# Output panels 2 to 15 multiplied in pairs by Strassen's scheme, with y's sums of tokens and x' made during the branch panels

## What is computed

```python
    x = first_block(...)                      # ends in rms_norm(x) * final_norm_g
    # second block
    ua = (ya * silu(za)) @ w_branch_a;  ub = ... @ w_branch_b;  uc = ... @ w_branch_c
    g = sigmoid(gate_logits.reshape(b, s, 3, D_MODEL))
    y = g[:, :, 0] * ua + g[:, :, 1] * ub + g[:, :, 2] * uc
    return x + y @ w_out
```

## Time and profile before

| | us |
|---|---|
| median of 3 runs | 2179.81 |
| lowest, highest | 2178.41, 2181.3 |
| the profiled execution | 2179.51 |
| its span, first to last instruction | 2178.1 |
| TensorE busy | 2145.9 (99% of the span) |
| VectorE busy | 1505.6 (69%) |
| ScalarE busy | 959.8 (44%) |
| gate pairs | about 697 to 1123 |
| branch panels | about 1840 to 2001 |
| output panels | about 2001 to 2178 |

### The profile page before, as it was taken

How to read it: one execution, slowest core, us unless ns; L and a number is a source line. 1 busy time by engine, 2 the same in 40 slices (tenths; PEclk the granted TensorE clock), 3 DMA queues, 4 the chain that set the end, 5 groups by cost and what they waited for, 6 DMA issues and landing times.

```text
span 2178.1 us, 34635 instructions
## 1 busy us (share of the span) xinstructions
PE 2145.9 (99%) x11672; PEld 1825.9 (84%) x11672; DVE 1505.6 (69%) x2524; ACT 959.8 (44%) x1631; POOL 60.6 (3%) x115
## 2 busy tenths in 40 slices
PE   8899999999999999999999999999999999999999
PEld 6788888788888999999997777778777888888887
DVE  5887877785658888888866666665767766665333
ACT  7533454433335444444444555555656554222221
POOL 0000000000000000000000000000000000000000
PEclk9999999999999999999999999999999999999999
DMA  9676523674443443343332222222222223554443
GB/s 356 238 262 224 182 95 99 226 268 142 146 144 131 144 141 125 121 141 129 118 112 88 87 87 87 87 87 78 74 82 68 88 88 117 169 168 152 145 145 112
DMA packets 83508, 302.21 MB, mean 139 GB/s; under 512 B 9285, under 2 KB 11717, under 8 KB 75217
## 3 DMA queue, kind: packets, MB, share of 16 engines
q1 hardware_dynamic: 71568, 258.24, 35.2%
q0 software_dynamic: 9104, 38.28, 5.1%
q10 hardware_dynamic: 2738, 4.47, 0.5%
HBM read 279.69 MB, written 21.26 MB: 138 GB/s over the span
## 4 chain that ended last, share of the span: by engine, by line
PE 78%; DVE 7%; ACT 5%; DVEq 4%; issue 3%; DMA 3%; ACTq 1%; SPq 0%
PE bank L417 18%; PE bank L419 18%; PE bank L418 18%; PE bank L1147 6%; PE bank L1149 6%; PE bank L1148 6%; DVE w_lo L411 3%; DMA w_raw<-stream 2%; ACT w_hi L401 2%; PE bank L540 1%; PE bank L571 1%; DVEq L406 1%; PE bank L553 1%; ACT L461 1%; ACT probs L614 1%
## 5 line engine op out<-in xcount | busy, mean ns | idle before, releaser
L417 PE MATMUL bank<-x_hi,w_hi 128*128 128x512 f32 x2224 | 886.2, 398 | 6.9 <-DVEq L668 1.9
L419 PE MATMUL bank<-x_hi,w_lo 128*128 128x512 f32 x2224 | 866.7, 390 | 0.0
L418 PE MATMUL bank<-x_lo,w_hi 128*128 128x512 f32 x2224 | 866.2, 389 | 0.0
L411 DVE TENSOR_TENSOR w_lo<-w_raw,w_hi 128x512 fp32r<-128x512 f32 x524 | 363.0, 693 | 495.0 <-ACT w_hi L401 473.6
L401 ACT ACTIVATE w_hi<-w_raw 128x512 fp32r<-128x512 f32 x524 | 331.2, 632 | 666.4 <-PE bank L419 554.0
L417 PEld LDWEIGHTS bank<-x_hi,w_hi 128*128 128x128 f32 x2224 | 417.6, 188 | 110.8 <-issue 11.1
L418 PEld LDWEIGHTS bank<-x_lo,w_hi 128*128 128x128 f32 x2224 | 417.9, 188 | 89.6 <-issue 6.0
L419 PEld LDWEIGHTS bank<-x_hi,w_lo 128*128 128x128 f32 x2224 | 417.5, 188 | 88.2
L1147 PE MATMUL bank<-x_hi,pw_hi 128*128 128x256 f32 x1176 | 332.9, 283 | 0.3 <-DVE pw_lo L1914 0.3
L1148 PE MATMUL bank<-x_lo,pw_hi 128*128 128x256 f32 x1176 | 332.8, 283 | 0.0
L1149 PE MATMUL bank<-x_hi,pw_lo 128*128 128x256 f32 x1176 | 332.8, 283 | 0.0
(11 more groups left out here) (193 smaller groups left out, 1812.0 us busy)
## 6 DMA issues: line engine op xcount, KB each, us to landing
w_raw<-stream SPq DMA_DIRECT2D x262, 512.0 KB, 3.8
pw_raw<-stream SPq DMA_DIRECT2D x84, 512.0 KB, 4.6
wmod<-w_mod_rows SPq DMA_DIRECT2D x32, 1024.0 KB, 7.1
front_raw<-stream SPq DMA_DIRECT2D x16, 1024.0 KB, 9.3
wmod<-w_mod_rows POOLq DMA_DIRECT2D x16, 1024.0 KB, 5.7
sig_store<-logits POOLq DMA_DIRECT2D x45, 256.0 KB, 2.5
sig_back<-sig_store SPq DMA_DIRECT2D x8, 768.0 KB, 5.6
gate_sig<-sig_store SPq DMA_DIRECT2D x7, 768.0 KB, 5.7
```

What stands on the lines that cost most here:

```text
L411: nc.vector.tensor_tensor(w_lo[:, q, :], raw_quarter(s), w_hi[:, q, :].bitcast(F32), ALU.subtract).then_inc(lo_ready, 1)
L417: nc.tensor.matmul(bank_ap[:, :tokens], hi, x_hi[:, kx, :], start=start, stop=False)
L418: nc.tensor.matmul(bank_ap[:, :tokens], hi, x_lo[:, kx, :], start=False, stop=False)
L419: return nc.tensor.matmul(bank_ap[:, :tokens], lo, x_hi[:, kx, :], start=False, stop=stop)
```

## The change

Output panels 0 and 1 stay as they were. Panels 2 to 15 are multiplied in 7 pairs by the same `product` that the gate pairs use, so the last stage is 2 panels and 49 products.

What the pairs need is made as follows. The sums of y's token blocks are made in place in x3: `sums_of_y(k)` for k = 0 to 6 stands in step 1 of the odd beats 3, 5, ... 15, and k = 7 at the start of the output stage; each is four VectorE operations of 128 x 256. They are split into x2 (8 ScalarE and 8 VectorE operations of 128 x 1024) during output panels 0 and 1. x' of tiles 2 to 15 is no longer made in the output stage: in each beat n = 2 to 15 SyncE loads x1's tile from DRAM into the one buffer `x_prime`, VectorE scales it there (`x_primed`, in step 2, behind branch(n, 0)), and GpSimd's queue stores it back to the same place. The load of tile n waits until tile n - 1 has been stored. Each result tile then takes two VectorE additions (`back_and`, and the bank).

```diff
-          ("gated", 4), ("branch", KT - 1), ("out", KT)]
+          ("gated", 4), ("branch", KT - 1), ("out", 2)]
...
+            def x_prime_load(n):
+
+                if n.lowest() > 2:
+                    sp.wait_ge(xp_stored, (n - 2).times(16).value())
                 else:
                     for stored in x1_stored:
                         sp.wait_ge(stored, 32)
+                sp.dma_start(x_prime[:, :], x_store[n.pick(), :, :].rearrange("a p t -> p (a t)")).then_inc(xp_loaded, 16)
+
+            def branch_loads(n, slot):
+
+                load_panel(sp, n + (FIRST["branch"] - 1))
+                sigmoid_loads(n, slot)
+                x_prime_load(n)
+            for slot in range(2):
+                branch_loads(At(2 + slot), slot)
+            with steps(sp, 1, KT // 2 - 1) as i:
+                for slot in range(2):
+                    branch_loads(At(2 + slot, 2, i), slot)
...
+            first = 4 * PAIRS
+            for n in range(2):
+                load_panel(sp, At(FIRST["out"] + n))
+            for n in range(2):
+                back_load(n)
+            for l in range(6):
+                load_factor(first + l)
+            sp.wait_ge(xp_stored, 16 * (KT - 2))
+            for p in range(OUT_PAIRS):
+                back_load(2 + 2 * p)
+                for l in range(4 * p + 6, min(4 * p + 8, 4 * OUT_PAIRS)):
+                    load_factor(first + l)
+                back_load(3 + 2 * p)
+                for l in range(4 * p + 8, min(4 * p + 10, 4 * OUT_PAIRS)):
+                    load_factor(first + l)
...
             panel(pe, At(g + 1), At(r + 1), x1_hi, x1_lo)
-            with steps(pe, 1, KT // 2) as i:
-                for n in range(2):
-                    panel(pe, At(g + n, 2, i), At(r + n, 2, i), x1_hi, x1_lo)
+            for l in range(PRODUCTS, PRODUCTS + 7 * OUT_PAIRS):
+                if l == PRODUCTS + 2:
+                    pe.wait_ge(t_ready, KT)
+                product(Factor(l))
...
+            g = FIRST["out"]
+            for s in range(8):
+                split_hi(act, At(4 * g + s))
+                token_sums_hi(KT // 2 + s)
+                if s == 5:
+                    store_result(0)
+                if s == 6:
+                    act.wait_ge(lo_ready, 4 * PANELS)
+                    factor_hi(Factor(PRODUCTS))
+                if s == 7:
+                    act.wait_ge(w_used, 4 * PANELS - 2)
+                    factor_hi(Factor(PRODUCTS + 1))
+            act.wait_ge(w_used, 4 * PANELS)
+            for l in range(PRODUCTS, PRODUCTS + 7 * OUT_PAIRS):
+                act_product(l)
+            store_result(KT - 1)
...
+            def x_primed(n):
+
+                dve.wait_ge(xp_loaded, (n - 1).times(16).value())
+                nc.vector.scalar_tensor_tensor(x_prime[:, :], x_prime[:, :], col("final_g", n), r_one[:, :],
+                                               ALU.mult, ALU.mult).then_inc(xp_made, 1)
+
+            def sums_of_y(k):
+
+                two = tile(x3, k.times(2) + 1)
+                one = tile(x3, k.times(2))
+                dve.drain()
+                nc.vector.tensor_tensor(one[:, HALF:], one[:, HALF:], one[:, :HALF], ALU.subtract)
+                dve.drain()
+                nc.vector.tensor_tensor(two[:, HALF:], two[:, HALF:], one[:, HALF:], ALU.subtract)
+                dve.drain()
+                nc.vector.tensor_tensor(two[:, :HALF], two[:, :HALF], two[:, HALF:], ALU.subtract)
+                nc.vector.tensor_tensor(one[:, :HALF], two[:, HALF:], one[:, :HALF], ALU.subtract)
+                dve.drain().then_inc(t_made, 1)
+
+            def branch_beat(n, slot, loaded, before, k=None):
 
                 for s in range(4):
...
+                    if s == 1 and k is not None:
+                        sums_of_y(k)
                     if s >= 2:
                         branch(n, s - 2, slot, loaded)
+                    if s == 2 and n.lowest() > 1:
+                        x_primed(n)
                     if s == 3:
                         low_part(n - 1, x1_hi, x1_lo, y_hi, y_split)
             branch_beat(At(1), 1, At(1), (0, None))
             with steps(dve, 0, KT // 2 - 1) as i:
                 branch_beat(At(2, 2, i), 0, At(1, 1, i), (1, At(1, 1, i)))
-                branch_beat(At(3, 2, i), 1, At(2, 1, i), (0, At(1, 1, i)))
+                branch_beat(At(3, 2, i), 1, At(2, 1, i), (0, At(1, 1, i)), At(0, 1, i))
...
+            def back_and(n, terms_so_far):
+
+                dve.drain()
+                dve.wait_ge(x_back_loaded[n % 2], 16 * (n // 2 + 1))
+                dve.wait_ge(result_stored[n % 2], 16 * (n // 2) + ONE)
+                nc.vector.tensor_tensor(result[:, n % 2, :].rearrange("p (a t) -> p a t", a=2), terms_so_far,
+                                        x_back[:, n % 2, :].rearrange("p (a t) -> p a t", a=2), ALU.add)
+                dve.drain()
+
+            def first_result(pair):
+
+                n = 2 + 2 * (pair.c - PAIRS)
+                back_and(n, pair_sum[:, :].rearrange("p (a t) -> p a t", a=2))
+                dve.wait_ge(product_done, 7 * pair.c + 5)
+                nc.vector.tensor_tensor(result[:, n % 2, :], result[:, n % 2, :], row_1[:, :], ALU.add).then_inc(row_read, 1)
+                dve.drain().then_inc(result_ready, 1)
...
+            sums_of_y(At(KT // 2 - 1))
+            for s in range(8):
+                split_lo(dve, At(4 * g + s))
+                if s > 0:
+                    token_sums_lo(KT // 2 + s - 1)
+                if s == 5:
+                    finish(0)
+                if s == 7:
+                    token_sums_lo(KT - 1)
+                    factor_lo(Factor(PRODUCTS))
+            weight_sum(Factor(PRODUCTS + 2))
+            factor_lo(Factor(PRODUCTS + 1))
+            for l in range(PRODUCTS, PRODUCTS + 7 * OUT_PAIRS):
+                dve_product(l)
+            second_result(At(PAIRS + OUT_PAIRS - 1), (PAIRS + OUT_PAIRS - 1) % 3)
...
+            with steps(pool, 0, KT - 2) as i:
+                n = At(2, 1, i)
+                pool.wait_ge(xp_made, (n - 1).value())
+                pool.dma_start(x_store[n.pick(), :, :].rearrange("a p t -> p (a t)"), x_prime[:, :]).then_inc(xp_stored, 16)
```

More of the change, by code:

```diff
@@ L53 @@
 PRODUCTS = 7 * PAIRS
+OUT_PAIRS = (KT - 2) // 2
 HALF = T // 2
@@ L994, in _ @@
             sigmoid_loads(At(1), 1)
-            with steps(sp, 0, KT // 2 - 1) as i:
-                for slot in range(2):
-                    load_panel(sp, At(FIRST["branch"] + 1 + slot, 2, i))
-                    sigmoid_loads(At(2 + slot, 2, i), slot)
-            def back_loads(n, slot, again=True):
-                src = x_store[n.pick(), :, :].rearrange("a p t -> p (a t)")
-                load_panel(sp, n + FIRST["out"])
-                if again:
-                    sp.wait_ge(result_ready, (n - 1).value())
+            def x_prime_load(n):
+                if n.lowest() > 2:
+                    sp.wait_ge(xp_stored, (n - 2).times(16).value())
                 else:
@@ L1907, in factor_lo @@
             def factor_lo(f):
-                if not f.exists():
+                if f is None:
                     return
@@ L2126, in finish @@
-                dve.wait_ge(result_stored[n.parity()], (n.half().times(16) + ONE).value())
-                nc.vector.tensor_tensor(result[:, n.parity(), :], acc[rr.parity()][:, :], back,
-                                        ALU.add).then_inc(result_ready, 1)
-                dve.drain().then_inc(acc_free[rr.parity()], 1)
-            def out_beat(n, peeled=False):
-                for s in range(4):
-                    split_lo(dve, (n + FIRST["out"]).times(4) + s)
-                    if s == 0 and not peeled:
-                        finish(n - 1)
@@ L2136, in _ @@
-            out_beat(At(0), peeled=True)
-            out_beat(At(1))
-            with steps(dve, 1, KT // 2 - 1) as i:
-                for slot in range(2):
-                    out_beat(At(slot, 2, i))
-            out_beat(At(KT - 2))
-            out_beat(At(KT - 1))
-            finish(At(KT - 1))
+                dve.wait_ge(w_used, 4 * (FIRST["out"] + n + 1))
+                nc.vector.tensor_tensor(result[:, n, :], acc[r % 2][:, :], back, ALU.add).then_inc(result_ready, 1)
+            def back_and(n, terms_so_far):
[5 more added lines that the diff above has]
+                dve.drain()
```

102 lines of the change are left out of this document (54 added, 48 removed).

## The result

The changed kernel takes 2216.5 us (2208.6 to 2217.4 in 4 runs) against 2179.2 (2178.4 to 2181.3 in 4): 1.014 times as long, with a 95% interval of 1.0119 to 1.0161. It is slower by 37 us, outside the predicted range of 2171 to 2197, near the time that rival B gives. The profiled execution took 2216.55 us, its span 2215.0.

A forecast was written before the change was run, and what follows sets the result against it. The prediction took TensorE as the bound: from the profiled 2179.5 us, -11.2 for products, +12.2 for the x' ring and +2.7 before the first product gave 2183.2, as a median 2183.5; range 2171 to 2197, likeliest 2178 to 2188.

The forecast's parts named there:

- rival B: Branch beats: x' stores land as x1's did, 4.8 us instead of 2.5; 2213 us, chance 0.1.
- What bounds the kernel now: Whole kernel: TensorE is most of the chain of waits; less matmul work is worth its full time unless something becomes late.
- Products instead of panels: Output stage: seven pairs at 2.88 us per product, 20.16 per pair against 21.76 for two panels; 11.2 us gained.
- Rival D: Output stage: products don't reach 2.88 us, 4.9 us lost per 0.1 us each; chance 0.18 together with C.
- The loop over x': Branch stage: 13 rings of waits through the one x' buffer take 154.0 us against 141.4 for 13 beats; TensorE loses 12.2.
- The ring: Branch beats: one x_primed to the next, via store and loads; 10.82 us even, 12.73 odd, against a beat of 10.88.
- From panels to products: Start of the output stage: TensorE ends its two panels and waits 2.7 us for factor 0; bounds 0.5 and 4.
- A: Branch beats: the ring doesn't bind, the half panel comes in time; 2171.3 us, chance 0.22 including rings losing under half.
- C: Branch beats: stores and loads cross, or GpSimd waits for VectorE's port; 2190 to 2193 us, chance 0.18 with D.

The follow-up runs named there:

- run 1: Changed kernel with SyncE issuing the first half of the next panel ahead of the x' load in each branch beat: 2178.9 us, 0.9994 of the kernel before.
- run 8: Changed kernel without an edit, profiled a second time: 2216.3 us, 1.0152 times the kernel before.
- run 2: Kernel before with only x' loaded, multiplied and stored back in the branch beats, in the changed kernel's order: 2202.0 us, 1.0092 times the kernel before.
- run 4: Changed kernel with x' made at the head of each branch beat, ahead of VectorE's four low splits: 2185.4 us, 1.0002 times the kernel before.
- run 5: Changed kernel with each branch beat's second half panel issued only when the first has landed, SyncE's loop written out: 2203.0 us, one run.

## Why the prediction was wrong

**What bounds the kernel now: right.** TensorE sets the time, less matmul work is worth its full length, and a wait in the branch stage costs its full length too.

**Products instead of panels: right.** 2.88 us per product was forecast. In run 1, 140.9 us from the first start to the last, 48.9 products: 2.88. In the changed kernel it is 142.4 / 48.9 = 2.91, with one stretch of 3.4 us at half clock, from 2069 (below). The same kernel in run 8 has no such stretch in its products and takes 140.9 again, so the stretch cost 1.5. Rival D is out. The first of each three matmuls in run 1, the changed kernel and run 8:

```profile
L1182 PE MATMUL bank<-x_hi,pw_hi x392: 278/283/388, 2037.9 to 2178.8; 128*128 128x256 f32 x196
```

```profile
L1176 PE MATMUL bank<-x_hi,pw_hi x392: 278/283/420, 2068.8 to 2211.2; 128*128 128x256 f32 x196
```

```profile
L1176 PE MATMUL bank<-x_hi,pw_hi x392: 283/283/387, 2071.8 to 2212.7; 128*128 128x256 f32 x196
```

**The loop over x': the mechanism was right, its size wrong, and this is the step that failed.** The term was +12.2, with bounds of 5.7 and 42 of which the range took in only the lower part; it measured +35.7. The ring binds, by the way the prediction went round it, and runs 1, 2 and 4 show it from three sides. The excess of 22.95 us over 154.0 splits over the 13 rings like this (sum of the forecast, sum measured):

| piece | forecast | changed kernel | excess |
|---|---|---|---|
| x' made to GpSimd's start | 3.8 | 9.3 | +5.5 |
| store landed, x' load issued | 34.7 | 31.1 | -3.6 |
| x' load issued to split of the half panel | 54.5 | 69.1 | +14.6 |
| split to next x' made | 61.1 | 67.5 | +6.4 |

- The store was right: from its start to SyncE's next issue it was 2.4 us on the mean where the forecast had 2.67. Rival B's time, 2213, was nearly right, but its cause, a store of 4.8, did not occur.
- GpSimd's start was taken from the earlier trace rows, where a store waited for ScalarE: 0.29. Here it is 0.66 to 0.94. The Trainium skill's rule of the shared port, which the prediction weighed, doesn't show: the store at 1918.43 began inside a split of VectorE's that ran from 1918.11 to 1918.80.
- The pair of x' load and half panel was taken from the earlier trace rows: 4.19. Here it is 5.31 on the mean: 0.71 from one issue to the other, where the row has 0.38, and 4.60 from there to the split, where it has 3.81. In the row the two halves were issued in 2.06 us. Here they take 0.91 in most odd rings, with 4.87 to the split on the mean, and 1.6 to 1.9 in the even ones, with 4.29, and the gates' load follows. With both behind the landing (run 5) the pair is 0.37 + 3.91 = 4.28, so the row was read rightly and carried over to a place where its condition didn't hold. In the odd rings the ring itself made that condition false: a late ring frees both halves before the first is issued. The estimate of 3.8 from the Trainium skill's formula, whose section describes transfers issued by GpSimd and not by SyncE, was further off than the row.
- The splits: 5.28 from the split to x' in odd beats instead of 4.83, and 3.12 instead of 2.92 in even ones without disturbance; the drain ahead of the sums (0.24 of idle time) was forgotten. From branch(n, 0) to x' it was 0.98 to 1.02 in all beats, where 0.85 was taken; the 0.80 that this leaned on stands in no row. In the changed kernel's even rings the way from the split to x' is up to 3.75, since the second split waits for TensorE, which the ring before had held up (0.44 at 1914.72).

How a size error of 15% in the ring became three times the loss: the forecast's even ring lay 0.06 under the beat, its odd one 1.85 over. What is lost is the ring less the beat. 1.77 us more on the mean ring, on an excess of 0.97, is all of it. The prediction saw for itself that 0.06 us per ring moved the result across 0.2% (it calls this a twentieth of B; it is a fortieth of B's 2.3). With every piece taken from an undisturbed place, 2178 to 2188 was too narrow a range for the likeliest case.

**From panels to products: right, 1.9 us instead of 2.7.** VectorE and ScalarE went as described, the split of the last sums waiting 3.34 behind the store; in run 1, where no ring holds up the panels ahead of it, TensorE's wait was 2.9. The end as a whole: -8.5 forecast, -6.5 in the changed kernel, -8.0 in the same kernel in run 8, -8.2 in run 1; the difference of 1.5 is that stretch at half clock.

**The first part: +7.8, put at nothing without a word, and open.** Without it the changed kernel would still be slower than the range: 2216.5 - 7.8 = 2208.7. Ahead of x1's first tile, 5.0 of 5.3 us are a longer wait of TensorE and, by the estimate above, a lowered clock; what makes the wait longer isn't known.

**Rivals.** A (2171) has its sum in run 1 only behind the first y: stage and end 7.4 us shorter than before, where A has 8.5. Its time, 2178.9, is not A's, by what is lost ahead of the first y. The lowered clock, which the prediction left out by intent, did come, at the end of each of the changed kernel's seven odd rings. C's range was passed by a mechanism near to its first half, transfers that cross.

## What to carry to other kernels

When a change closes a ring of waits through a single buffer, its excess over the beat is paid in every turn, so where a ring comes out within a tenth of the beat, as here, an error of that size in its pieces decides the result: look whether one order of issue takes a link out, before working on its length. And put the load that the bound engine needs ahead of any load that waits for a store: here the order of two issues on SyncE was worth 35 us of the stage. Durations from an undisturbed place hold only while their spacing holds; ask whether the new wait itself brings transfers together.

## What the runs showed of the hardware

TensorE's granted clock fell from 2.4 to 1.2 GHz for stretches of 3.4 us although TensorE had only short waits. In the changed kernel there were eight such stretches between 1877 and 2072, and each began during one of its waits for VectorE or at most 1.3 us behind it, of 2.75, 3.16, 3.91, 3.73, 4.37, 3.31, 2.22 and 1.88 us. The fifth, with the stretch of time around it:

```profile
1987.62 0.80 PE L420 MATMUL bank<-x_hi,w_hi 128*128 128x512 f32 x1 [4.37 <-DVEq L2119]
```

```profile
1987.00:1989.00 2.00, 1.38 (x3) 1.16 (x4) 1.54 (x3) 0.00 (x0) 0.00 (x0) 0.55 0.00 0
```

A matmul takes 0.80 there where 0.39 is usual. The length of the wait alone doesn't decide: behind the 1.88 us at 2068.84 the clock fell, behind run 1's wait of 2.91 it didn't (1.00 from 2034 to 2042), nor in run 2 with its twelve waits of up to 1.9. Even the same wait of the same kernel goes both ways: the one that ends at 1838.07 in the changed kernel took 1.88 us, with the clock at 1.00 from 1836 to 1841; in run 8 it took 1.87, ended at 1835.15, and the clock was at 0.50 from 1836 to 1839. What decides was not tested. In the branch stage the rings add up to the whole loss, so the pace is theirs, and most of what the clock costs TensorE there seems to be hidden; in the products it cost 1.5 us, by run 8.
